# Three vector parts, late side weights, early shift parameters and two earlier weight halves in a two-layer decoder on one core

## The reference

```python
h = rms_norm(x, mix_norm[l])
proj = h @ w_in                       # in_proj[l]; from layer 1 on also vres_down
p_rwkv = token_shift(proj[..., :RWKV_COLS], shift_mu[l])   # p + (prev - p) * mu
r, k, v, d_w, d_a, d_g = jnp.split(p_rwkv, RWKV_SPLITS, axis=-1)
w_log = -softplus(-(w0 + tanh(d_w) @ w_up)) - 0.5
a = sigmoid(a0 + d_a @ a_up)
g = sigmoid(d_g) @ g_up
kk = heads(k * k_k)                   # "scaled keys"
kk = kk * rsqrt(maximum(sum(kk * kk, -1, keepdims=True), 1e-24))
k = k * (1 + (a - 1) * k_a)
# then the recurrence over tokens, in parallel differential attention on the other columns
```

## Time and profile before

| | us |
|---|---|
| median of 3 runs | 1915.58 (1913.62 to 1916.8) |
| the profiled execution | 1913.58 |
| its span | 1911.7 |
| PE busy | 1825.6 (95%) |
| DVE busy | 1492.5 (78%) |
| ACT busy | 1172.8 (61%) |
| POOL busy | 74.6 (4%) |

### The profile page before, as it was taken

The page is one execution under the profiler, slowest core; times in us unless marked ns, Lnnn a source line. Parts: engine busy times, 40 slices in busy tenths (PEclk is TensorE's granted clock), DMA queues, the critical chain, the costliest instruction groups (busy, mean ns, idle before and its releaser), DMA issues.

```text
span 1911.7 us, 31576 instructions
## 1 busy us (share of the span) xinstructions
PE 1825.6 (95%) x10589; PEld 1418.7 (74%) x10589; DVE 1492.5 (78%) x2051; ACT 1172.8 (61%) x1576; POOL 74.6 (4%) x110
## 2 busy tenths in 40 slices
PE   6899998999988999988999999999999999999998
PEld 5555577888865565677788888888888888888886
DVE  5854776655567556765999999989999999999997
ACT  4432454554544123453887787887787788877875
POOL 4100000000030000000200000000000000000000
PEclk9999999999999999998999999999999999999999
DMA  8431262665653322534999999999999999999993
GB/s 260 153 107 62 80 207 89 189 187 187 188 154 118 120 64 68 165 110 165 325 381 337 362 361 348 370 338 362 356 347 369 352 348 381 332 364 348 361 370 140
DMA packets 224012, 474.51 MB, mean 248 GB/s; under 512 B 16680, under 2 KB 41400, under 8 KB 223376
## 3 DMA queue, kind: packets, MB, share of 16 engines
q1 hardware_dynamic: 219456, 458.29, 68.2%
q0 software_dynamic: 3472, 13.65, 2.2%
q10 hardware_dynamic: 960, 1.10, 0.2%
HBM read 468.25 MB, written 1.05 MB: 245 GB/s over the span
## 4 chain that ended last, share of the span: by engine, by line
PE 54%; DVE 1%; issue 0%; ACT 0%; DVEq 0%
PE psum L472 16%; PE psum L474 16%; PE psum L473 16%; PE psum L1012 2%; PE psum L1059 1%; PE psum L1023 0%; PE psum L1024 0%; PE psum L883 0%; PE psum L871 0%; PE psum L496 0%; ACT hN L1287 0%; PE psum L581 0%; ACT SH L1479 0%; PE psum L1104 0%; DVE x L2236 0%
## 5 line engine op out<-in xcount | busy, mean ns | idle before, releaser
L472 PE MATMUL psum<-w_hi,h_hi 128*128 128x512 f32 (+1 forms) x1552 | 613.2, 395 | 33.2 <-DVE w_lo L426 26.6
L474 PE MATMUL psum<-w_hi,h_lo 128*128 128x512 f32 (+1 forms) x1552 | 605.6, 390 | 0.0
L473 PE MATMUL psum<-w_lo,h_hi 128*128 128x512 f32 (+1 forms) x1552 | 605.4, 390 | 0.0
L472 PEld LDWEIGHTS psum<-w_hi,h_hi 128*128 128x128 f32 x1552 | 293.9, 189 | 103.1 <-DVE w_lo L426 21.1
L474 PEld LDWEIGHTS psum<-w_hi,h_lo 128*128 128x128 f32 x1552 | 293.8, 189 | 62.5
L473 PEld LDWEIGHTS psum<-w_lo,h_hi 128*128 128x128 f32 x1552 | 294.4, 190 | 59.0 <-issue 0.2
L426 DVE SCALAR_TENSOR_TENSOR w_lo<-ring,col,w_hi 128x512 fp32r<-128x512 f32 (+1 forms) x184 | 130.9, 758 | 77.1 <-ACT w_hi L412 76.2
L442 DVE TENSOR_TENSOR w_lo<-ring,w_hi 128x1024 fp32r<-128x1024 f32 x144 | 172.4, 1221 | 7.6 <-ACT w_hi L438 3.2
L438 ACT ACTIVATE w_hi<-ring 128x1024 fp32r<-128x1024 f32 x144 | 151.9, 1060 | 41.0 <-PE psum L474 41.0
L412 ACT ACTIVATE w_hi<-ring,col 128x512 fp32r<-128x512 f32 (+1 forms) x184 | 118.7, 697 | 94.4 <-PE psum L474 76.5
L442 DVE TENSOR_TENSOR w_lo<-dproj,w_hi 128x1024 fp32r<-128x1024 f32 x120 | 145.9, 1222 | 17.3 <-ACT w_hi L438 14.0
(11 more groups left out here) (324 smaller groups left out, 2454.7 us busy)
## 6 DMA issues: line engine op xcount, KB each, us to landing
ring<-in_expert_w_gu SPq DMA_DIRECT2D x128, 512.0 KB, 5.3
SH<-in_expert_w_gu SPq DMA_DIRECT2D x120, 512.0 KB, 5.9
proj<-in_expert_w_gu SPq DMA_DIRECT2D x104, 512.0 KB, 6.3
dproj<-in_expert_w_gu SPq DMA_DIRECT2D x72, 512.0 KB, 6.0
dproj<-in_expert_w_down SPq DMA_DIRECT2D x72, 512.0 KB, 5.1
ring<-in_expert_w_down SPq DMA_DIRECT2D x64, 512.0 KB, 5.2
ring<-in_in_proj SPq DMA_DIRECT2D x48, 512.0 KB, 4.6
ring<-in_dense_w_gu SPq DMA_DIRECT2D x88, 256.0 KB, 3.1
```

The source lines that it names most:

```text
L472: pe.matmul(o, h[0], w[0], start=start, stop=False, skip_group_check=True)
L473: pe.matmul(o, h[0], w[1], start=False, stop=False, skip_group_check=True)
L474: return pe.matmul(o, h[1], w[0], start=False, stop=stop, skip_group_check=True)
```

## The change

The vectors are reordered so that the key scale comes first, and divided into three parts: `kk_s` alone (256 KB), decay bias, iclr bias and `ka_s` (768 KB), and the rest (1280 KB), with a semaphore each. In layer 0 POOL loads the first where part 0 was and the third where part 1 was; SP loads the second at block 14, ahead of the tables there. The side weights and `scol` are loaded last, after the V shift, with a semaphore of their own (`side_in`). For layer 1 `mu` is loaded as soon as layer 0's last sums of squares (ahead of the dense part) are done; the unused output of the mixer's squares therefore goes to `dproj`. On ACT the high halves of blocks 12 and 13 are made before the wait for the scaled keys instead of after; on DVE the low half of block 12 before the scaled keys and that of block 13 before the reduction.

```diff
@@ -38,7 +38,7 @@
 
 VEC = {}
 _at = 0
-for _n, _w in (("decay_b", RW), ("iclr_b", RW), ("kk_s", RW), ("ka_s", RW), ("bonus", RW),
+for _n, _w in (("kk_s", RW), ("decay_b", RW), ("iclr_b", RW), ("ka_s", RW), ("bonus", RW),
                ("gn_w", RW), ("gn_b", RW), ("vres_b", RW), ("q_norm", DQ), ("k_norm", DQ), ("lq1", DQ), ("lq2", DQ),
                ("lk1", DQ), ("lk2", DQ), ("subln", DV)):
     VEC[_n] = (_at, _w)
@@ -199,6 +199,7 @@
         PT = nbf[:, 8192:9216].rearrange("p (s n) -> p s n", s=2)
         qn = dproj[:, :, :].rearrange("p t c -> p (t c)")[:, 0:2048].rearrange("p (t c) -> p t c", t=TT)
         qTx = hT[:, :].rearrange("p (k t) -> p k t", k=KD)
+        x_junk = dproj[:, :, :].rearrange("p t c -> p (t c)")[:, 0:2048].rearrange("p (t c) -> p t c", t=TT)
         on = SH[:, 0:2048].rearrange("p (t c) -> p t c", t=TT)
         px = SH[:, 2048:3072].rearrange("p (s q k) -> p s q k", s=2, q=2)
 
@@ -287,8 +288,9 @@
         mu_in, scol_in = sem("mu_in"), sem("subln_columns_in")
         x_in_s = [sem(f"x_in{g}") for g in range(2)]
         ident_in, col_in = sem("ident_in"), sem("columns_in")
-        small_in, vec_in, mem_in_s, out_s = sem("small_in"), sem("vec_in"), sem("mem_in"), sem("out_s")
-        lw_in = sem("layer_weights_in")
+        small_in, vec_in, mem_in_s, out_s = sem("small_in"), [sem(f"vec_in{q}") for q in range(3)], sem("mem_in"), sem("out_s")
+        first_vec_in = sem("first_vec_in")
+        lw_in, side_in = sem("layer_weights_in"), sem("side_weights_in")
         dve_step, act_step, pool_step = sem("dve_step"), sem("act_step"), sem("pool_step")
         sq_done = sem("squares_done")
         msq_done, mn_done = sem("mem_squares_done"), sem("mem_scale_ready")
@@ -313,7 +315,7 @@
             return w[k0 * P:(k0 + 2) * P, c0:c0 + cw].rearrange("(k p) n -> p k n", p=P)
         chunks_in = [(512, 512), (1536, 256), (0, 512), (1024, 512), (1792, 512), (2304, 512), (2816, 512)]
         K_, LORA_, R_, V_, VR_ = range(5)
-        VEC_PARTS = [slice(0, VEC["bonus"][0]), slice(VEC["bonus"][0], NV)]
+        VEC_PARTS = [slice(0, RW), slice(RW, VEC["bonus"][0]), slice(VEC["bonus"][0], NV)]
         shift_cols = chunks_in[0:4] + [(RC, VR)]
 
         IN_TURN = [(c, kb) for c in range(4) for kb in range(0, KD, 2)]
@@ -600,7 +602,7 @@
                 some(in_steps, 7)
                 if l:
                     pe.wait_ge(raw_ready, 2 * 8)
-                    pe.wait_ge(lw_in, 80)
+                    pe.wait_ge(side_in, 32)
                     for t in range(TT):
                         bank = B.open(pe, ("vr", l, t), nproj[0] % 4)
                         nproj[0] += 1
@@ -614,7 +616,7 @@
                     pe.wait_ge(lora_ready, l + 2)
                     transposes(("vt", l), [pv[:, t, RC:RC + VR] for t in range(TT)])
                 some(in_steps, 2)
-                pe.wait_ge(lw_in, 80 + 64 * l)
+                pe.wait_ge(lw_in, 48 + 64 * l)
                 B.wait_evacuated(pe, ("lt", l))
                 for t in range(TT):
                     ts = slice(t * P, (t + 1) * P)
@@ -1126,6 +1128,7 @@
             sp.dma_start(cst[:, 0:P], consts[:, 0:P]).then_inc(ident_in, 16)
             for n, (kind, src, cw, _) in enumerate(blocks):
                 if n == 14:
+                    sp.dma_start(vec[:, VEC_PARTS[1]], vecs[0, VEC_PARTS[1]].partition_broadcast(P)).then_inc(first_vec_in, 16)
                     sp.dma_start(cst[:, P:], consts[:, LEVELS.stop:]).then_inc(small_in, 16)
                     sp.dma_start(hT[:, 0:5 * P], consts[:, LEVELS]).then_inc(small_in, 16)
                     for c in range(2):
@@ -1218,8 +1221,10 @@
                     pool.wait_ge(block_in[RING - 1], arrived[RING - 1])
                 else:
                     pool.wait_ge(ycat_df, l)
-                    for cs in VEC_PARTS:
-                        pool.dma_start(vec[:, cs], vecs[l, cs].partition_broadcast(P)).then_inc(vec_in, 16)
+                    for q, cs in enumerate(VEC_PARTS):
+                        pool.dma_start(vec[:, cs], vecs[l, cs].partition_broadcast(P)).then_inc(vec_in[q], 16)
+                    pool.wait_ge(sq_done, 2 * 3 * l)
+                    pool.dma_start(mu, mus[l].partition_broadcast(P)).then_inc(mu_in, 16)
                     B.wait_evacuated(pool, ("wo", l - 1, 1, 1))
                 pool.dma_start(lora_w[0:64, :], decay_up[l]).then_inc(lw_in, 16)
                 pool.dma_start(lora_w[64:128, :], iclr_up[l]).then_inc(lw_in, 16)
@@ -1230,16 +1235,12 @@
                 pool.memset(prev[0:1, 0, :], 0.0).then_inc(row0_ready, 1)
                 if l:
                     gained_x(l)
-                pool.wait_ge(sq_done, 2 * 3 * l + TT)
-                pool.dma_start(mu, mus[l].partition_broadcast(P)).then_inc(mu_in, 16)
+                if l == 0:
+                    pool.wait_ge(sq_done, TT)
+                    pool.dma_start(mu, mus[l].partition_broadcast(P)).then_inc(mu_in, 16)
                 shift_in(l, K_)
                 if l == 0:
-                    for w_, s in ((vresd_w[:, :, :], vres_down[0].rearrange("(k p) n -> p k n", p=P)),
-                                  (router_w[:, :, :], router[0].rearrange("(k p) n -> p k n", p=P))):
-                        pool.dma_start(w_, s).then_inc(lw_in, 16)
-                    for q in range(DEPTH):
-                        pool.dma_start(scol[:, q:q + 1], vecs[q:q + 1, a:a + w].rearrange("l p -> p l")).then_inc(scol_in, 16)
-                    pool.dma_start(vec[:, VEC_PARTS[0]], vecs[0, VEC_PARTS[0]].partition_broadcast(P)).then_inc(vec_in, 16)
+                    pool.dma_start(vec[:, VEC_PARTS[0]], vecs[0, VEC_PARTS[0]].partition_broadcast(P)).then_inc(vec_in[0], 16)
                 shift_in(l, LORA_)
                 if l == 0:
                     gained_x(l)
@@ -1247,8 +1248,14 @@
                     shift_in(l, VR_)
                 shift_in(l, R_)
                 if l == 0:
-                    pool.dma_start(vec[:, VEC_PARTS[1]], vecs[0, VEC_PARTS[1]].partition_broadcast(P)).then_inc(vec_in, 16)
+                    pool.dma_start(vec[:, VEC_PARTS[2]], vecs[0, VEC_PARTS[2]].partition_broadcast(P)).then_inc(vec_in[2], 16)
                 shift_in(l, V_)
+                if l == 0:
+                    for w_, s in ((vresd_w[:, :, :], vres_down[0].rearrange("(k p) n -> p k n", p=P)),
+                                  (router_w[:, :, :], router[0].rearrange("(k p) n -> p k n", p=P))):
+                        pool.dma_start(w_, s).then_inc(side_in, 16)
+                    for q in range(DEPTH):
+                        pool.dma_start(scol[:, q:q + 1], vecs[q:q + 1, a:a + w].rearrange("l p -> p l")).then_inc(scol_in, 16)
                 pool.wait_ge(rk_read, l + 1)
                 pool.dma_start(mem_raw, mem_in[0].rearrange("(t p) d -> p t d", p=P)).then_inc(mem_in_s, 16)
 
@@ -1303,12 +1310,12 @@
                     split_to(3)
                 direct_hi(("hT", l, 0), 1)
                 split_to(base + 4)
-                squares(x, hNv, sm[:, 32:34], sq_done)
+                squares(x, x_junk, sm[:, 32:34], sq_done)
                 split_to(base + 6)
                 act.wait_ge(row_ready, 3 * l + 1)
                 for g in (K_, LORA_) + ((VR_,) if l else ()) + (R_,):
                     if g == R_:
-                        split_to(base + 12)
+                        split_to(base + 14)
                         act.wait_ge(kk_in, l + 1)
                         act.activation(NB[:, ECP, :], NB[:, KK, :], ACT.Square).then_inc(kk_sq, 1)
                     c0, cw = shift_cols[g]
@@ -1688,7 +1695,7 @@
                 row_scale(l, 0)
                 split_to(base + 6)
                 if l:
-                    dve.wait_ge(lw_in, 80)
+                    dve.wait_ge(side_in, 32)
                     dve.tensor_tensor(router_w[:, :, :], router_w[:, :, :], bc(gains(l, "ffn").unsqueeze(2), KD, NE), MUL).then_inc(side_ready, 1)
                 split_to(base + 8)
                 dve.wait_ge(mu_in, 16 * (l + 1))
@@ -1720,22 +1727,23 @@
                 for m in [lora_mix] + ([vr_mix] if l else []):
                     next(m)
                     next(m)
-                dve.wait_ge(vec_in, 32 * l + 16)
+                split_to(base + 13)
+                dve.wait_ge(vec_in[0], 16 * (l + 1))
                 dve.tensor_tensor(nb(KK), k_v, bc(V("kk_s").unsqueeze(1), TT, RW), MUL).then_inc(kk_in, 1)
-                split_to(base + 12)
+                split_to(base + 14)
                 dve.wait_ge(kk_sq, l + 1)
                 total(ss[:, 0:16], heads(NB[:, ECP, :]))
-                split_to(base + 13)
                 ts(ss[:, 0:16], ss[:, 0:16], 1e-24, None, ALU.max)
                 rs = rsqrt(ss, 16, 1.0, 0.0)
                 tt(heads(kkf), heads(kkf), bc(rs.unsqueeze(2), 16, HD), MUL)
                 split_to(base + 15)
 
+                dve.wait_ge(vec_in[1] if l else first_vec_in, 16)
                 for t in range(TT):
```

(4 more changed lines are left out.)

## The result

The changed kernel takes 1905.3 us, median of 8 runs (1903.37 to 1910.96), against 1915.42 us for the kernel before in the runs beside it (8 runs, 1913.62 to 1917.77): ratio 0.995, interval 0.9938 to 0.9963, that is 9.6 us faster (7.1 to 11.9) by the ratio; the two medians are 10.1 us apart. The forecast was 1901.5 us; the time lies inside its range of 1896 to 1909, 3.8 us above the predicted one.

What follows compares the result with a forecast made beforehand. TensorE, busy 95%, was taken as the bound, so time could come only from its idle or low-clock stretches at the layers' starts: 6.5 + 8.2 - 0.7 - 0.5 = 13.5, rounded to 13 us, forecasting 1901.5 us (1896 to 1909, 8 in 10).

Steps and rivals of the forecast that it cites:

- rival 1: Both layers' loads: they do not come earlier, so those gains go and the time is 1907 us; chance 0.13.
- rival 2: PE idling between low-rank products falls to 1.2 GHz ahead of V in both layers: 4.5 us lost, 1906 us; chance 0.15.
- three signs of being wrong: Blocks 10 and 11 still flying 11 to 14 us; clock 0.5 at block 14; ACT waiting for block 14 behind vectors.
- (a): Layer 0: smaller vector load and side weights off POOL's queue there land block 10 earlier, 3.0 us (2.5 to 3.8).
- (b): Layer 0: earlier halves of blocks 12 and 13 remove DVE waits, 1.1 us before the reduction, 2.4 us at low-rank products.
- (c): Layer 0: middle vector part on SP's queue and later side loads cost nothing; extra semaphores some tenths at most.
- (d): Layer 1: shift parameters loaded early, about 355 us, so block 9 lands and PE starts R sooner, 2.7 us (0 to 3.2).
- (e): Layer 1: the new order removes DVE waits before the reduction and at low-rank products: 1.1 + 3.1 + 0.8 + 0.5 = 5.5 us.
- (f): Costs, both layers: POOL slowing moved DVE work, 0.7 us (0 to 1.2); low clock ahead of block 14, 0.5 us.
- Rival 3: Fewer low-clock stretches ahead of block 10 and the whole 4.7 us earlier landing count: 17 us, 1897.5 us; chance 0.14.
- 4: Slower: late block 13 in layer 0 holds square, reduction and R copies; 20 us beyond gives some 1920 us; chance 0.03.
- 5: Nothing reaches the end: V's shift or the memory-token load ends last anyway; within 3 us, 1914 us; chance 0.06.

## Why the prediction was right and wrong

The sum was 13.5, rounded to 13; the whole change gave 9.6 (7.1 to 11.9). That the time fell inside the range says little for the mechanism: the range had been drawn wide enough for rivals 1 and 2, and 1905.3 is nearer to their 1907 and 1906 than to the forecast of 1901.5. One of the three signs of being wrong came, the clock of 0.5 at block 14, in both layers of the first profile. The other two did not: blocks 10 and 11 fly 7.9 and 8.3 us, and ACT has block 14 without a wait. One term came out at nothing, others were too small and too large, and part of the agreement is luck.

**(a) Loads of layer 0, 3.0 us: wrong, nothing.** This is the step that failed. Not the landings: they are earlier, 8.3 us the longest flight instead of 14.1, so rival 1's number for this term came, but not its reason. What failed is the step from DVE's wait to the time, for an earlier low half meets a DVE that POOL's products hold up. Two measurements show the nothing: the loads alone 0.9995, and 1905.34 against 1905.27 us without and with them. The term read ACT's 4.41 us wait, and DVE's 3.84, as the price of the vector load and made its bounds (2.5 to 3.8 us) from them; that landing was the latest of six with the same loads, and their spread of 4.2 us is larger than the term. A part of a landing's delay is also lost on the way: block 10's low half at S + 17.3 (the shift parameters alone) and S + 21.5 (before) is followed by the scaled keys 12.5 and 11.0 us later, since POOL's products lie beside more of the early mixes (2.31 and 1.95 us each) than of the late ones (1.75 and 1.52).

**(b) Order in layer 0, 3.5 us: right in kind, the size in part luck.** The biases stand at 46.8 us in the mean of the five profiles with the old order (45.0 to 48.2) and at 43.4 in that of the four with both halves ahead and nothing else altered on PE or POOL (43.2 to 43.6): 3.4 us. But three of the five have block 10 late, at 19.2 to 20.0, and none of the four. Among profiles with like landings the order brings 1.6 us (45.0 with block 10 at 15.9, 43.4 with it at 16.0) and 2.1 (45.7 at 16.9, 43.6 at 17.05). What it brings at a late landing no profile shows. The waits of 1.12, 0.44, 1.19 and 0.77 us are gone, as said. The split was wrong too: block 13 was priced at the 1.1 us ahead of the reduction, and without it the whole change is worth nothing (1.0002).

**(c) Vector part on SP, at nothing: right.** ACT waits 0.20 us for block 12 (39.12) and 4.62 us before block 13's high half (45.08), the latter for PE, not for a landing; no wait for the vector part or for block 14 behind it appears.

**(d) Shift parameters, 2.7 us: right in kind, too small.** The K mix comes at 25.4 instead of 29.0 us, 3.6 us; the whole kernel gains 4.4 (2.5 to 6.5). PE restarts R without a wait, and 3.6 is close to the cap of 3.5 us that the prediction worked out from PE's own work and above the 2.7 that it took from the bytes. PE's clock at the restart was forecast at 1.0 and is low.

**(e) Order in layer 1, 5.5 us: the waits yes, the end no.** The biases come at 48.3 instead of 51.1 us with `mu` early, at 51.3 instead of 54.7 or 56.1 without: 2.8 to 4.8, where the terms up to there (1.1 and 3.1) were 4.2. At the lambda product the order gives 0 in the profile of the order alone (76.4 against 76.0 and 77.4) and in the changed kernel (73.0 against 72.4 with `mu` alone), and 3.6 where the clock stayed up (68.8).

**(f) Against it, 0.7 and 0.5 us: both mis-sized.** The clock is rival 2, priced at 2.5 us a layer. It had a chance of 0.15; it came in layer 1 in four of the five profiles that have both halves ahead and neither filling nor interleaving, and cost more, 4.1 us, because not only the twelve matmuls of block 14 but also the second tile's products run at half speed (2.07 for 1.12 us); in layer 0 it came in the changed kernel's first profile (66.0 against 64.4 us at the tables, 1.6 us), not in its second nor with the order alone, and with POOL late or one half only. Contention was priced only as what the change would add, 0 to 1.2 us. What POOL takes from DVE ahead of the scaled keys is 4.5 us in all; the kernel before paid most of it too, so it added little to the time; but 1.5 us of what an earlier block 10 gives went to it (12.5 against 11.0 us, above). The row was there: the earlier trace rows show a pair at 2.41 us with POOL at work and at 1.42 without. The rule weighed there, of the Trainium skill ("SBUF — State Buffer", Who interferes with whom), that a VectorE instruction with two inputs in SBUF contends with GpSimd's reads, holds here and for more forms: 1.22 us became 2.30 and 1.41 became 2.60 in such pairs, and a group of 0.38 on 16 elements 2.21.

By measured terms: 0 for the loads, 1.8 us at the tables in layer 0 at like landings (66.0 to 64.3) up to 4.3 against before's own two profiles with the late one (68.7 and 68.5 to 64.4), 3.6 for the shift parameters, and 0 to 3.6 for the order in layer 1 depending on the clock, 5.4 to 11.5 us. The kernel's 9.6 lies between, but a span so wide tests little. Rival 3 did not come: its earlier landings did, but they were worth nothing. Nor did 4: the reduction starts 35.5 us after the first sum of squares (54.93 - 19.47), 35.2 before (53.26 - 18.01). Nor 5: the time reached the end.

**What stays open.** Between the level tables and the start of layer 1, where all kernels do the same, the profiles differ by 3 us: 455.2 to 455.3 in three (before, the shift parameters alone, the filling), 456.4 to 456.8 in five, 457.9 to 458.4 in six (before's second profile and the changed kernel's two among them). It follows no part of the change. Why the clock falls in layer 1 in one execution and not in the next is open too; what is shown is that with PE at work throughout it did not fall, in the one profile of each of the two kernels.

## What to carry to other kernels

A wait for a landing in one profile is worth at most what the next item behind it can give, and may be that execution's own: before pricing a load that leaves a queue, see whether the engine behind it is held by something else as well. When work is brought forward so that an engine gets ahead of its supplier, bring forward the whole run up to the next real work, or put real work into the new pauses: here both blocks gave 4.2 us, one block of two took back all that the change had gained, and 6.1 us more came from spreading the blocks between the dependent products. Filler products kept the clock up but stood in the way of the products they were to help.

## What the runs showed of the chip beyond what was expected

- The mean granted clock tells executions of one kernel apart: the kernel without the new loads took 1901.69 us at 0.989, 1905.34 at 0.986 and 1910.41 at 0.984.
- POOL beside DVE stretches small instructions most: two of 128x16 took 2.21 us instead of 0.38, two mixes of 128x1024 2.30 and 1.94 us instead of 1.22.
- The same order of loads makes block 10 available 15.9 to 20.0 us after the first sum of squares, from one profile to the next; with 1024 KB and 160 KB beside it cut to 256 KB it is 16.5 to 17.8 in eight profiles.
- PE stayed at the high level through pauses of 0.71 and 0.75 us between products in one execution, and in another fell to the low one behind a pause of 0.75 us; a low stretch of some 10 us followed (granted 0.60 from 590 to 592, 0.50 from 592 to 600).
